# The first half of the input projection in three passes of rounded halves, with two jobs moved from VectorE and GpSimd to ScalarE

## What is computed

```python
proj = rmsnorm(x) @ w_in                       # 1024 inputs; 44 tiles of 128 outputs
q, k, v, z, xbc, dt = split(proj)
attn = softmax(mask(q @ k.T)) @ v              # per head, 16 heads
xs, B, C = silu(causal_conv(xbc, 4 taps))      # 12 of the 44 tiles
h = h * exp(sum(dt*a)) + B * to_end * x        # state, prompt and samples
y = (C @ h ...) * silu(z)
out = concat(rmsnorm(attn), rmsnorm(y)) @ w_out
... = peer_ffn(out)                            # product keys, 16384 experts
```

## Time and profile before

| | |
|---|---|
| runs | 1176.15, 1177.0, 1177.91 us; median 1177.0 |
| profiled execution, span on its core | 1177.8 us, mean granted TensorE clock 0.994 |
| busy in the span | PE 1145.5 us (97%), DVE 793.4 (67%), POOL 758.9 (64%), ACT 569.8 (48%) |
| tiles 2 to 43 | 21.57 to 226 us |
| chain that ended last | PE 71% of the span, all other engines 1% or less each |

### The profile page before, as it was taken

The page is one execution under the profiler, slowest core; times in us unless marked ns, Lnnn a source line. Parts: engine busy times, 40 slices in busy tenths (PEclk is TensorE's granted clock), DMA queues, the critical chain, the costliest instruction groups (busy, mean ns, idle before and its releaser), DMA issues.

```text
span 1177.8 us, 24286 instructions
## 1 busy us (share of the span) xinstructions
PE 1145.5 (97%) x7599; PEld 1012.2 (86%) x7599; DVE 793.4 (67%) x1718; ACT 569.8 (48%) x1289; POOL 758.9 (64%) x642
## 2 busy tenths in 40 slices
PE   8999999989999999999999999999999999999997
PEld 7887777758888999999999999998888887888876
DVE  6789788874299997002899999984454466665534
ACT  3323223544354555565555554445555555555545
POOL 0066443237355998988666666676677797789754
PEclk9999999999999999999999999999999999999999
DMA  7468667695443666656544455545666697788653
GB/s 249 143 231 280 195 194 221 207 344 175 152 155 109 199 186 185 187 172 189 143 144 139 141 143 144 144 143 153 187 188 189 189 325 252 224 281 291 191 153 108
DMA packets 108667, 225.13 MB, mean 191 GB/s; under 512 B 12754, under 2 KB 21570, under 8 KB 108074
## 3 DMA queue, kind: packets, MB, share of 16 engines
q1 hardware_dynamic: 104706, 210.50, 57.5%
q0 software_dynamic: 2944, 10.49, 2.6%
q10 hardware_dynamic: 936, 3.14, 0.7%
HBM read 215.80 MB, written 8.19 MB: 190 GB/s over the span
## 4 chain that ended last, share of the span: by engine, by line
PE 71%; issue 1%; DVE 1%; POOL 0%; ACT 0%; DVEq 0%; POOLq 0%; ACTq 0%
PE bank L1689 31%; PE bank L1719 30%; PE bank L1699 5%; PE bank L1642 2%; PE bank L1654 1%; PE bank L1666 1%; DVE hl L2092 0%; PE bank L1739 0%; PE bank L1756 0%; POOL hl L1582 0%; DVE acts L2115 0%; PE bank L1747 0%; ACT acts L1925 0%; POOL hl L1567 0%; PE bank L1774 0%
## 5 line engine op out<-in xcount | busy, mean ns | idle before, releaser
L1567 POOL TENSOR_TENSOR hl<-ring,hl 128x512 fp32r<-128x512 f32 x448 | 585.5, 1317 | 187.5 <-ACT hl L1805 180.5
L1805 ACT CAST hl<-ring 128x512 fp32r<-128x512 f32 x512 | 317.1, 620 | 292.1 <-PE bank L1719 161.7
L1689 PE MATMUL bank<-split,hl 128*128 128x256 f32 x3072 | 378.5, 282 | 0.4 <-ACT hl L1805 0.3
L1689 PEld LDWEIGHTS bank<-split,hl 128*128 128x128 f32 x3072 | 366.3, 189 | 0.8 <-issue 0.5
L1719 PE MATMUL bank<-hl,split 128*128 128x512 f32 x1524 | 353.9, 394 | 1.9 <-DVE hl L2092 1.9
L1719 PEld LDWEIGHTS bank<-hl,split 128*128 128x128 f32 x1524 | 286.2, 188 | 69.7 <-DVE hl L2092 2.4
L533 PE MATMUL pj<-xn,ring 128*128 128x264 f32 x672 | 158.5, 392 | 0.7 <-ACT proj L824 0.7
L2085 DVE TENSOR_TENSOR split<-acts,split 128x256 fp32r<-128x256 f32 x128 | 128.3, 1028 | 40.0 <-ACT split L1901 37.0
L533 PEld LDWEIGHTS pj<-xn,ring 128*128 128x128 f32 x672 | 126.4, 192 | 24.7 <-issue 4.6
L2092 DVE TENSOR_TENSOR hl<-ring,hl 128x512 fp32r<-128x512 f32 x64 | 49.9, 779 | 115.6 <-ACT hl L1805 115.6
L2051 DVE TENSOR_SCALAR bv<-bkey,ig 128x130 f32<-128x130 f32 x256 | 86.0, 394 | 0.0
(11 more groups left out here) (369 smaller groups left out, 1107.1 us busy)
## 6 DMA issues: line engine op xcount, KB each, us to landing
ring<-in_uv SPq DMA_DIRECT2D x256, 256.0 KB, 2.7
ring<-in_v_rows SPq DMA_DIRECT2D x256, 256.0 KB, 3.1
ring<-in_w_ring SPq DMA_DIRECT2D x76, 512.0 KB, 4.2
room<-in_cache_k SPq DMA_DIRECT2D x64, 128.0 KB, 2.8
hs<-in_state_ssm SPq DMA_DIRECT2D x8, 512.0 KB, 4.7
out_ssm_s<-hs SPq DMA_DIRECT2D x8, 512.0 KB, 6.3
acts<-x_rows SPq DMA_DIRECT2D x8, 512.0 KB, 4.7
room<-in_cache_v SPq DMA_DIRECT2D x12, 256.0 KB, 5.7
```

The costliest lines, as they stand in the source:

```text
L1567: nc.gpsimd.tensor_tensor(hl[:, r % HL, 1], raw[:, r], hl[:, r % HL, 0].bitcast(F32), ALU.subtract).then_inc(lo_done, 1)
L1689: mm = nc.tensor.matmul(out, hl[:, r % HL, m, k * P:(k + 1) * P], split[:, x, kk, 0:TP], start=(kk == 0 and n == 0), stop=(kk == KD - 1 an ...
L1805: nc.scalar.copy(hl[:, r % HL, 0], raw[:, r]).then_inc(hi_done, 1)
```

## The change

The first 512 inputs (blocks 0 to 3) of tiles 2 to 43 go through the three-pass form, blocks 4 to 7 stay float32. ACT rounds the 128x512 half of a tile into `wi` (`in_high`, directly behind the `copy` of the tile two places before), POOL subtracts and writes the remainder over the weights in the ring (`in_low`). The input's halves are `x_high` (ACT) and `x_low` (DVE), made once. The first tap of the convolution of tiles 4 to 11 goes from DVE to ACT (`tap`), the scaling of the probabilities from DVE to ACT (`normal`; DVE keeps the reciprocals), the decay of the states from POOL to ACT (`decay_state`, eight instructions a pair instead of four). DVE's product `xdt` stands ahead of pair 0. The small arrays `acs`, `dth`, `rffn` and `ig` get other places in memory. The core of the diff:

```diff
@@ -192,13 +192,16 @@
         sb("proj_end", [P, PROJ - K0, NT], where=st)
-        dth = sb("dth", [NH, NT], where=st)
         tail_s = sb("tail_s", [P, CONV_CH, NB, CONV_W - 1], where=st)
         tail_p = sb("tail_p", [P, CONV_CH, CONV_W - 1], where=st)
-        acs = sb("acs", [NH, TP], where=st)
         tokh = sb("tokh", [P, TT, 3, NH], where=st)
         dd = sb("dd", [NH, 2, NB], where=st)
-        xn = sb("xn", [P, KD, NT], where=st)
+        with ExitStack() as early:
+            xn = sb("xn", [P, KD, NT], where=early)
+        x_low = sb("x_low", [P, KD // 2, NT], F32R, where=st)
+        sb("xn_end", [P, KD // 2, NT], where=st)
+        x_high = sb("x_high", [P, KD // 2, NT], F32R, where=st)
+        wi = sb("wi", [P, 2, PIECE], F32R, where=st)
         wdt = sb("wdt", [P, KD, NH], where=st)
...
@@ -458,19 +464,21 @@
             def _(pool):
+                def in_low(i):
+
+                    r = 2 * (i % RING)
+                    pool.wait_ge(w_hi, i - 1)
+                    nc.gpsimd.tensor_tensor(ring_lo[:, r], raw_o[:, r], wi[:, i % 2].bitcast(F32), ALU.subtract).then_inc(w_lo, 1)
+
+                for i in range(2, CONV_CH):
+                    in_low(i)
                 pool.wait_ge(normed, 2)
                 pool.wait_ge(early_out, 2)
                 nc.gpsimd.memset(q6w.rearrange("p a b n -> p (a b n)"), 0.0).then_inc(zeroed, 1)
-                pool.wait_ge(dds_done, 1)
-                pool.wait_ge(xdt_done, 1)
                 for c in range(KD):
                     s, g = c % HS, c * GROUPS // KD
-                    pool.wait_ge(hs_full[s], 16 * (c // HS) + 16)
-                    for h in range(HALF, NB + HALF, HALF):
-                        b = slice(h - HALF, h)
-                        dec = nc.gpsimd.tensor_tensor(hs[:, s, b], hs[:, s, b], dds[:, c, 0, b].unsqueeze(2).broadcast_to([P, HALF, P]),
-                                                      ALU.mult)
-                    dec.then_inc(decayed, 1)
+                    in_low(CONV_CH + 4 * c)
+                    pool.wait_ge(xdt_done, 1)
                     pool.wait_ge(bc_in, 16)
...
@@ -478,12 +486,15 @@
                     fed_in.then_inc(fed, 1)
+                    in_low(CONV_CH + 4 * c + 1)
                     pool.wait_ge(decayed, c + 1)
                     pool.wait_ge(fed, c + 1)
                     for h in range(HALF, NB + HALF, HALF):
                         b = slice(h - HALF, h)
                         sums = nc.gpsimd.tensor_tensor(hs[:, s, b], hs[:, s, b], up[:, b], ALU.add)
                     sums.then_inc(st_done, 1)
+                    in_low(CONV_CH + 4 * c + 2)
+                    in_low(CONV_CH + 4 * c + 3)
 
...
@@ -525,12 +536,21 @@
                         pe.wait_ge(pj_copied, i - 1)
-                    for k in range(KD):
+                    for k in range(0 if i < 2 else 4, KD):
                         if i == 0:
                             pe.wait_ge(xg_done, k + 1)
-                        if i == 2 and k % 4 == 0:
-                            pe.wait_ge(normed, k // 4 + 1)
-                        mm = nc.tensor.matmul(pj[i % 2][:, 0:NT], ring[:, s, k], (xg if i < 2 else xn)[:, k], start=(k == 0), stop=(k == KD - 1))
+                        if i == 2 and k == 4:
+                            pe.wait_ge(normed, 2)
+                        mm = nc.tensor.matmul(pj[i % 2][:, 0:NT], ring[:, s, k], (xg if i < 2 else xn)[:, k], start=(k == (0 if i < 2 else 4)),
+                                              stop=(i < 2 and k == KD - 1))
+                    for kind in range(3 if i >= 2 else 0):
+                        if i == 2 and kind < 2:
+                            pe.wait_ge((x_his, x_los)[kind], 1)
+                        pe.wait_ge(w_lo if kind == 2 else w_hi, i - 1)
+                        for k in range(4):
+                            w = ring_lo[:, 2 * s, k * P:(k + 1) * P] if kind == 2 else wi[:, i % 2, k * P:(k + 1) * P]
+                            mm = nc.tensor.matmul(pj[i % 2][:, 0:NT], w, (x_low if kind == 1 else x_high)[:, k],
+                                                  start=False, stop=(kind == 2 and k == 3))
                     mm.then_inc(ring_used[s], 1)
...
@@ -817,11 +837,29 @@
 
+                def in_high(i):
+
+                    act.wait_ge(ring_full[i % RING], 16 * (i // RING) + 16)
+                    nc.scalar.copy(wi[:, i % 2], raw_o[:, 2 * (i % RING)]).then_inc(w_hi, 1)
+
+                in_high(2)
+                in_high(3)
+
+                def tap(i):
+
+                    act.wait_ge(pj_copied, i + 1)
+                    act.wait_ge(silu_done, i - 1)
+                    c = CT[i]
+                    nc.scalar.activation(cv[:, i % 2], proj[:, c, 0:TP], ACT.Copy, scale=par[:, P_CW + c * CONV_W + 3:P_CW + c * CONV_W + 4]
+                                         ).then_inc(tapped, 1)
+
                 def copy(i):
 
                     at = CT[i] if i < CONV_CH else (Q0, K0, V0, Z0)[(i - CONV_CH) % 4] + (i - CONV_CH) // 4
                     act.wait_ge(ring_used[i % RING], i // RING + 2)
                     nc.scalar.copy(proj[:, at, :], pj[i % 2][:, 0:NT]).then_inc(pj_copied, 1)
+                    if i + 2 < N_IN:
+                        in_high(i + 2)
 
...
@@ -876,6 +914,8 @@
                 nc.scalar.activation(par[0:NH, P_ALOG:P_ALOG + 1], par[0:NH, P_ALOG:P_ALOG + 1], ACT.Exp).then_inc(dt_b, 1)
+                act.wait_ge(normed, 1)
+                nc.scalar.copy(x_high[:], xn[:, 0:4]).then_inc(x_his, 1)
                 copied_early(1)
...
@@ -907,9 +949,30 @@
                     copy(i)
+                    tap(i)
                     silu(i - 1)
                 silu(CONV_CH - 1)
                 silu_samples(1)
+
+                def decay_state(c):
+
+                    s = c % HS
+                    act.wait_ge(hs_full[s], 16 * (c // HS) + 16)
+                    act.wait_ge(dds_done, 1)
+                    for b in range(NB):
+                        ins = nc.scalar.activation(hs[:, s, b], hs[:, s, b], ACT.Copy, scale=dds[:, c, 0, b:b + 1])
+                    ins.then_inc(decayed, 1)
+
+                decay_state(0)
+
+
+                def normal(c):
+
+                    for j in range(2):
+                        act.wait_ge(recips_done, 2 * c + j + 1)
+                        nc.scalar.activation(sc[:, j, 0:P], sc[:, j, 0:P], ACT.Copy, scale=stat[:, j, 4:5])
+                        nc.scalar.activation(sc[:, j, P:3 * P], sc[:, j, P:3 * P], ACT.Copy, scale=stat[:, j, 5:6]).then_inc(p_ready, 1)
+
                 def spread(c):
...
@@ -941,6 +1004,8 @@
                     copy(CONV_CH + 4 * c)
+                    if c:
+                        normal(c - 1)
                     decays(c)
...
@@ -955,6 +1020,8 @@
                     copy(CONV_CH + 4 * c + 3)
+                    if c < KD - 1:
+                        decay_state(c + 1)
 
...
@@ -1065,7 +1133,10 @@
                         dve.wait_ge(silu_done, i - 1)
-                    link(nc.vector.tensor_scalar(to, proj[:, c, 0:TP], cw[3], None, ALU.mult))
+                    if i < 4:
+                        link(nc.vector.tensor_scalar(to, proj[:, c, 0:TP], cw[3], None, ALU.mult))
+                    else:
+                        dve.wait_ge(tapped, i - 3)
                     for j in (1, 2):
...
@@ -1096,6 +1167,8 @@
                                             ).then_inc(normed, 1)
+                dve.wait_ge(x_his, 1)
+                nc.vector.tensor_tensor(x_low[:], xn[:, 0:4], x_high[:].bitcast(F32), ALU.subtract).then_inc(x_los, 1)
                 conv(0)
...
@@ -1246,24 +1319,20 @@
 
-                def normal(c):
+                def recips(c):
 
                     for j in range(2):
                         dve.wait_ge(expd, 2 * c + j + 1)
-                        link(nc.vector.reciprocal(stat[:, j, 4:6], stat[:, j, 2:4]))
-                        nc.vector.tensor_scalar(sc[:, j, 0:P], sc[:, j, 0:P], stat[:, j, 4:5], None, ALU.mult)
-                        nc.vector.tensor_scalar(sc[:, j, P:3 * P], sc[:, j, P:3 * P], stat[:, j, 5:6], None, ALU.mult
-                                                ).then_inc(p_ready, 1)
-
+                        nc.vector.reciprocal(stat[:, j, 4:6], stat[:, j, 2:4]).then_inc(recips_done, 1)
+
+                dve.wait_ge(silus_done, 2)
+                dve.wait_ge(dds_done, 1)
+                nc.vector.tensor_tensor(xdt[:], proj[:, X0:X0 + KD, TP:NT], dds[:, :, 1], ALU.mult).then_inc(xdt_done, 1)
                 for c in range(KD):
                     if c:
                         sample_out(c - 1)
-                        normal(c - 1)
+                        recips(c - 1)
                     ssd_in(c)
-                    if c == 0:
-                        dve.wait_ge(silus_done, 2)
-                        dve.wait_ge(dds_done, 1)
-                        nc.vector.tensor_tensor(xdt[:], proj[:, X0:X0 + KD, TP:NT], dds[:, :, 1], ALU.mult).then_inc(xdt_done, 1)
```

16 lines of the change are left out of this document (12 added, 4 removed).

## The result

The changed kernel takes **1180.3 us** (median of 17 runs, 1176.0 to 1185.3), the kernel before 1177.0 (17 runs, 1173.7 to 1180.9). The ratio is 1.0036, 95% interval 1.0024 to 1.0048: slower by 4 us, where 11 us less was forecast. It also lies outside the range. The profiled execution of the change has a span of 1181.7 us, 3.9 over that of before.

A forecast was written before the change was run, and what follows sets the result against it. PE was taken to bound most of the stretch, DVE where POOL disturbs it. A -13.4, B -4.3, C +2.1, D +4.0, E +0.5 sum to -11.1 us: 1166.0 us against the median of 1177.0, range 1157 to 1176.

The forecast's parts named there:

- A, TensorE's work: Tiles 2 to 43: each takes 3.24 us, 0.32 less, by float32r records; times 42 tiles, -13.4 us.
- B, pairs 1 to 7: Waits in pairs 1 to 7: 0.8 us left a pair, 5.6 against 9.9 us, so -4.3 us.
- The rival in which POOL disturbs DVE in every pair: Pairs 1 to 7 each take the 22.4 us of pair 1: slower, 1187 us; chance 0.10.
- C, start: Start: `x_low` in DVE's chain makes tile 5 start 1.2 us later, hiding the gain of tiles 2 to 4: +2.1 us.
- D, pair 0: Pair 0: POOL's remainders queue behind `up`; stalls of 3.1 us in tile 13, then 0.9 us: +4.0 us, bounds 0 and 6.
- E, the tail: After the pairs: POOL's squares and sums end later, both units of values are issued late: +0.5 us, bounds -1 and +3.
- Clock: Drops to 1.2 GHz, as at tile 7: 1.8 us an event; one may be added or removed; in the range only.

The follow-up runs named there:

- the moves alone: The kernel before with fourth taps, scaling of the probabilities and decay of the state moved to ScalarE, no split, all tiles float32: 1173.2 us, ratio 0.9959.
- the filler: Matmuls of no use in TensorE's waits: the change with 14 (tile 5) and 12 (tile 13), 1182.7 us, ratio 1.0062; in other kernels, in the tail.

## Why the prediction was wrong

Against the profiled span the forecast was 1166.7 us and the measured one 1181.7, so 15 us are missing: 0.9 ahead of tile 2, 3.5 in tiles 2 to 11, 1.0 in pair 0, 2.4 in pairs 1 to 7 and 8.4 in the tail, less 1.2 in the rest. By its own steps:

- **A, TensorE's work: right in size.** 3.24 us a tile as forecast. Between the moves alone and the change a pair's four tiles differ by 1.15 us (13.45 against 14.60 in pair 3), where I had 1.28; over seven pairs that is 0.9 us less.
- **B, pairs 1 to 7: right in mechanism, 2.4 us short** (0.9 of it A's). The waits of before went; new ones of about 0.85 us a pair, for ACT's scaling, came in their place (forecast 0.8, "turn_probs ... 0.5 us late" among it). The rival in which POOL disturbs DVE in every pair fell here: pair 1 took 18.4 us, not 22.4.
- **C, start: the wait 0.7 us short, the clock behind it missing.** Tile 5 was to be 1.2 us late and was 2.8, of which 0.9 were there at tile 2 already. Tiles 2 to 11 took 44.86 us instead of the 41.3 forecast. 2.8 us of that are the half clock in tile 5. In profiles without any half clock there, with the filler and in the kernel with the unit of values earlier, they took 40.4 us; the forecast of 41.3 holds the half clock that the kernel before has at tile 7.
- **D, pair 0: right.** Stalls of 2.83 and, in the second profile of the change, 1.06 us, against 3.1 and 0.9. The step was 1.0 us short in all (4.0 forecast), by DVE beside POOL and by the clock. It put no wait on the landing of `bcb`; in the two profiles of the change `xdt` came later and that cost nothing, in two others it did.
- **E, the tail: the step that failed.** I had +0.5 us, bounds -1 to +3, and it was +8.9 (+7.9 in the second profile). I had priced only how late the second unit of values would be issued, and even that too low: six us less the 2.24 of slack is 3.8, not 1.5 to 3, and counted from the end of the pairs it came 9.6 us later, not 6. Three things were left out. The first unit moved as well, from 206.6 to 228.2 us, as it stands in the same list behind squares that now come after the last remainder. The squares themselves run beside DVE's closing chain and slow it. And some of the waits are followed by work at half clock. The late list alone gives 5.5 us (kernel before with one wait more); the squares and the first unit back inside the pairs take 6.6 off the change (91.9 to 85.3). The last 2.4 us over the 83.0 are in every kernel with the moves and early squares (85.45 without the split, where TensorE is done earlier and waits 3.6 us for DVE's rounded mix; with the filler there the tail was 82.5).
- **Clock: in the range with 1.8 us an event, not in the sum.** That was the second mistake. Over many runs, one less the mean granted clock (0.987 for the change in 17 runs, 0.992 for before in the 93 runs of the later comparisons) times twice the span gives 31 and 19 us at 1.2 GHz. Half a microsecond lost for each makes 6 us of difference: more than the whole of the loss. Without it the change would be 1.3 us faster than before (1163.3 against 1164.6 us of span). This is an estimate, and it holds only as far as TensorE bounds while the clock is low; the filler at the start, which didn't pay, shows that it does not always.

The rule of the Trainium skill ("TensorE: Matmul & The Clock Gate", section "Terms") puts the penalty at the throttled time times one half. From tile 5 to tile 8 the change had 10.2 us and 6.8 us at 1.2 GHz in its two profiles, which by the rule cost 5.1 and 3.4. Against the profiles with filler they cost 4.4 and 3.3. So the trace agrees within 0.7 us, and 0.9 us of the first stretch lay in the idle time ahead of tile 5, where it cost nothing.

The other rule of the Trainium skill, that of "SBUF — State Buffer", section "SBUF: two separate sides" (one of the two engines is blocked for the other's whole instruction), which I had weighed for the pairs only, bears on pair 0 and the tail. The trace agrees in kind: beside POOL's squares DVE's products of 264 columns take 0.84 us instead of 0.43. In size it goes further than one instruction of the other engine: one of the eight L1382 took 3.18 us instead of 0.48 while POOL did two subtractions in a row, 2.50 us together. I read the rule at the engine that was busiest and not where DVE was last.

## What to carry to other kernels

An engine that gets more work in a loop pushes back what stands behind the loop in its list. Follow that work to its new time and look at what runs beside it and who waits for it; it may have had its place where it disturbed nobody. And price a new stall of TensorE with the clock that it brings: here a stall of 3.2 us cost 2.8 and 1.6 us more right behind it in the two profiles of the change, and nothing in three other kernels. Before adding arithmetic that is cheaper, try the freed schedule alone: here the three kernels with the moves to ScalarE and no split gained 0.4, 0.3 and 0.1%, and the three with a late start of the split and the squares inside the pairs 0.4 to 0.5%. Only the one with 0.1%, that with filler, lies apart.

## What the runs showed that I had not expected

- The same stall does not always bring the half clock: behind 2.83 us of idle time in tile 13 the eight float32 records took 2.87 us in one profile of the change, and in the other no stretch of 1.2 GHz is near; behind the 3.2 us at the start it came in five profiles of eight. Runs of one kernel spread, 1176 to 1185 us for the change, with mean granted clocks of 0.983 to 0.990.
- Behind the filler the clock was at 2.4 GHz, except once, where another wait of 2.6 us followed it. At TensorE's wait for the rounded mix, half clock followed in seven of eight profiles without filler and in neither of the two with it. In the median the filler paid at most once in four kernels.
- The last eight products `mix<-mix,par,att` of DVE take 3.42 us, or 5.56 and 6.02 us, by where POOL's first two subtractions of output weights fall among them.
